# First layer of a two-layer attention and expert model on one core: q and k feature-major by head pairs, attention between projections, modulation sums on three engines and in layer two

## The reference, cut to what matters

```python
mod = c_act @ ada_w[layer] + ada_b[layer]            # 1024 x 6144 in each layer
sh_a, sc_a, g_a, sh_f, sc_f, g_f = split(mod, 6)
h = rmsnorm(x) * (1 + sc_a) + sh_a
# layer 0, 8 heads, two components of width 64 in each:
q, k, v = split(h @ w_qkv, 3)                        # each 512 x 1024
q, k = rmsnorm of every 64 columns, with gains
p[c] = softmax(q[c] @ k[c].T / 8 + bias[head], causal)
o = rmsnorm((p[0] - lam * p[1]) @ v) * (1 - lam_init)
x = x + g_a * (o @ w_o)
# layer 1: keys and values from their own modulation (kv_ada_w, 1024 x 2048), dilated attention
x = x + g_f * moe(rmsnorm(x) * (1 + sc_f) + sh_f)    # both layers: 2 of 32 experts for a token
```

## Time and profile before

| | us |
|---|---|
| median of 3 runs | 2227.99 |
| lowest, highest | 2224.74, 2230.22 |
| the profiled execution | 2229.98 |
| its span, first to last instruction | 2228.3 |

### The profile page before, as it was taken

The page is one execution under the profiler, slowest core; times in us unless marked ns, Lnnn a source line. Parts: engine busy times, 40 slices in busy tenths (PEclk is TensorE's granted clock), DMA queues, the critical chain, the costliest instruction groups (busy, mean ns, idle before and its releaser), DMA issues.

```text
span 2228.3 us, 16930 instructions
## 1 busy us (share of the span) xinstructions
PE 1804.4 (81%) x6253; PEld 825.3 (37%) x6253; DVE 694.2 (31%) x1078; ACT 449.1 (20%) x1002; POOL 131.5 (6%) x153
## 2 busy tenths in 40 slices
PE   1899767496899988998739999976869989998873
PEld 0433234345343333332224344443534433333321
DVE  5577567574100000000050255554330000000003
ACT  2111044302212111111030044441211111111100
POOL 0000010000100000000000000000000100000000
PEclk9999967696899999999969999996869999999996
DMA  7588730144699999999922112032038999999994
GB/s 279 205 332 308 263 118 19 60 151 165 220 351 394 392 388 384 391 380 391 396 103 76 38 38 76 26 126 97 38 125 304 398 395 387 388 379 381 392 389 176
DMA packets 243306, 552.62 MB, mean 248 GB/s; under 512 B 13328, under 2 KB 26209, under 8 KB 243222
## 3 DMA queue, kind: packets, MB, share of 16 engines
q1 hardware_dynamic: 221056, 501.24, 60.6%
q0 software_dynamic: 20624, 47.25, 6.0%
q10 hardware_dynamic: 1542, 3.01, 0.4%
HBM read 546.12 MB, written 32.59 MB: 260 GB/s over the span
## 4 chain that ended last, share of the span: by engine, by line
PE 55%; DMA 20%; DVE 14%; ACT 5%; issue 4%; SPq 0%; ACTq 0%; DVEq 0%; POOL 0%; POOLq 0%; PEldq 0%
PE psum L1818 22%; DMA ring<-in_moe_w_up_dram 17%; PE psum L1489 8%; PE psum L1849 7%; PE psum L1736 4%; PE psum L1535 4%; DVE W L1039 3%; PE psum L1561 2%; PE psum L1800 1%; ACT ring L715 1%; PE psum L1757 1%; DVE W L958 1%; DVE W L1126 1%; DVE small L1130 1%; PE psum L1455 1%
## 5 line engine op out<-in xcount | busy, mean ns | idle before, releaser
L1818 PE MATMUL psum<-ring,V 128*64 128x512 f32 (+1 forms) x2048 | 628.3, 630 | 92.8 <-DMA ring<-in_moe_w_up_dram 75.8
L1818 PEld LDWEIGHTS psum<-ring,V 128*64 128x64 f32 (+1 forms) x2048 | 239.8, 162 | 448.1 <-issue 447.9
L1849 PE MATMUL psum<-ring,V 128*64 128x512 f32 (+1 forms) x1024 | 305.5, 600 | 15.3 <-issue 10.4
L851 ACT ACTIVATE V<-psum,mods,scls 128x128 f32<-128x128 f32 x336 | 126.2, 456 | 525.8 <-PE psum L1800 525.8
L1489 PE MATMUL psum<-ring,HT 128*128 128x512 f32 x384 | 169.4, 596 | 0.0
L1849 PEld LDWEIGHTS psum<-ring,V 128*64 128x64 f32 (+1 forms) x1024 | 107.5, 154 | 157.7 <-issue 157.7
L1350 DVE TENSOR_TENSOR V<-V,psum 128x512 f32<-128x512 f32 x42 | 28.9, 688 | 408.0 <-PE psum L1818 408.0
L958 DVE SCALAR_TENSOR_TENSOR W<-ring,cact,W 128x512 f32<-128x512 f32 x196 | 147.4, 752 | 7.0
L1363 DVE COPY HT<-psum 128x512 f32<-128x512 f32 x42 | 29.1, 692 | 319.4 <-PE psum L1849 319.4
L1356 DVE COPY V<-psum 128x512 f32<-128x512 f32 x42 | 29.0, 691 | 290.5 <-PE psum L1829 290.5
L1039 DVE RECIPROCAL W<-W 128x512 f32<-128x512 f32 x24 | 80.5, 3353 | 115.3 <-ACT W L705 115.3
(11 more groups left out here) (253 smaller groups left out, 1508.7 us busy)
## 6 DMA issues: line engine op xcount, KB each, us to landing
ring<-in_moe_w_gate_dram SPq DMA_DIRECT2D x64, 2048.0 KB, 20.5
ring<-in_moe_w_up_dram SPq DMA_DIRECT2D x64, 2048.0 KB, 19.7
ring<-in_moe_w_down_dram SPq DMA_DIRECT2D x64, 2048.0 KB, 19.1
ring<-in_ada_w_dram SPq DMA_DIRECT2D x24, 2048.0 KB, 13.5
ring<-in_a_w_qkv_dram SPq DMA_DIRECT2D x6, 2048.0 KB, 19.3
ring<-in_kv_ada_w_dram SPq DMA_DIRECT2D x4, 2048.0 KB, 13.7
V<-expert_rows POOLq DMA_DIRECT2D x8, 1024.0 KB, 7.1
ring<-in_kv_w_dram SPq DMA_DIRECT2D x3, 2048.0 KB, 21.5
```

What stands on the lines that cost most here:

```text
L851: ins = act.activation(V[:, 2 * D + b * D + k * P:2 * D + b * D + (k + 1) * P], bank[0][:, q * P:(q + 1) * P], ACT.Identity, bias=mod[:, 2 ...
L1818: ins = pe.matmul(bank[2 + 2 * i + b][half * w:(half + 1) * w, :], V[:, col:col + w], slot3(x)[:, k, :], start=(k == 0), stop=(k == KC - 1))
L1849: ins = pe.matmul(bank[6 + hf][half * w:(half + 1) * w, :], V[:, col:col + w], slot3(x, 4)[:, k, hf * HALF:(hf + 1) * HALF], start=(k == 0 ...
```

## The change

**Before the loop.** SP no longer waits for the vectors. x is loaded by POOL's queue, first of all. Modulation blocks 0 to 3 are summed by TensorE: products of 32 columns by 512, four of them side by side in the columns of the array, then ACT copies the 128 x 512 and four products of one column each give the modulation as columns. All modulation goes this way now: the DRAM round trip and the row copies are gone. The bias rows go to DRAM and back without waiting for the modulation.

**Layer one** becomes 30 iterations n, written out. Iterations 0 to 23 have a unit each: for each pair of heads p (n = 6p to 6p+5) k and q of one head, two units of values, k and q of the other. q and k come out feature-major, as in layer two (mean square by a product, square root, reciprocal of 128 x 512), and never go to DRAM. Twenty attention steps of 512 score columns each (one or two (head, chunk) segments, `segments`) stand at n mod 6 = 3, 4, 0, 1, 2. A step's scores are made at n, its transposes at n+1, its values at n+2. There is one buffer for scores, one for probabilities and one for transposed ones. The per-head norm and the transposes of its outputs are done pair by pair, and parts of the output projection stand in iterations 24 to 28. Modulation blocks 4 to 19 are summed in the loop, ten by DVE and six by POOL (15 instructions for a block), each with its own accumulator; their products of one column stand at fixed iterations (`REDUCE_AT`).

**Layer two.** The remaining eight modulation blocks are loaded as 16 halves of 1024 x 256 into slot 5 and summed by DVE beside the 12 value units; `half_reduce` puts two products of one column each for a half in TensorE's queue.

**Gates.** POOL makes a diagonal of the gate's columns, a product with ones makes the row, ACT copies it; the DRAM broadcasts are gone.

The core of the diff; the removed code is the code before that the sections above name:

```diff
+UNITS0, STEPS0 = 24, 20
+SEGMENTS = [[(0, 3)], [(0, 2), (0, 0)], [(0, 1), (1, 1)], [(1, 2), (1, 0)], [(1, 3)]]
+STEP_AT = {6 * p + at: 5 * p + i for p in range(4) for i, at in enumerate((3, 4, 6, 7, 8))}
+
+
+N_MOD0 = 20
+N_HALF = 2 * (N_MOD - N_MOD0)
+ON_POOL = [5, 8, 10, 12, 14, 16]
+ON_DVE = [i for i in range(4, N_MOD0) if i not in ON_POOL]
+SUM_AT = dict(zip((0, 1, 2, 5, 8, 11, 14, 17, 20, 23), ON_DVE))
+REDUCE_AT = {at + 1: [i] for at, i in SUM_AT.items()}
+for at, i in zip((4, 7, 8, 10, 13, 16), ON_POOL):
+    REDUCE_AT[at] = REDUCE_AT.get(at, []) + [i]
+REDUCED = [i for at in sorted(REDUCE_AT) for i in REDUCE_AT[at]]
+HALVES_AT = [[i for i in range(N_HALF) if i * 3 // 4 == u] for u in range(12)]
...
+def segments(x):
+
+    out, at = [], 0
+    for half, c in SEGMENTS[x % 5]:
+        out.append((2 * (x // 5) + half, c, at, (c + 1) * P))
+        at += (c + 1) * P
+    return out
...
+    mods = [("mod", 0, i) for i in range(N_MOD0)]
+    order = mods[0:4] + [("kq", 0, 0), ("v", 0, 0)] + mods[4:7] + [("kq", 0, 1)] + mods[7:10] + [("kq", 0, 2)]
+    order += mods[10:13] + [("v", 0, 1)] + mods[13:15] + [("kq", 0, 3)] + mods[15:19] + [("wo", 0, 0)] + mods[19:]
+    order += [("wo", 0, 1)]
+    slots = [{"mod": i if i < 4 else (i - 4) % 3, "kq": (4, 3)[i % 2], "v": 5, "wo": 4 + i}[kind] for kind, _, i in order]
...
+    order += [("v", 1, 0), ("v", 1, 1), ("v", 1, 2)] + [("half", 1, i) for i in range(4)] + [("kq", 1, 0)]
+    slots += [0, 1, 2, 5, 5, 5, 5, 0]
+    order += [("half", 1, i) for i in range(4, 9)] + [("kq", 1, 1)] + [("half", 1, i) for i in range(9, N_HALF)]
+    slots += [5] * 5 + [1] + [5] * (N_HALF - 9)
+    order += [("kq", 1, i) for i in range(2, 2 * GROUPS)] + [("wo", 1, 0)]
+    slots += [2, 0, 1, 2, 0]
...
-            sp.wait_ge(vec_in, 16 * N_VEC)
...
+            pool.dma_start(x3, t["x"][0].rearrange("(c p) n -> p c n", p=P)).then_inc(x_in, 16)
...
+                def gate_diag(to, cols):
+
+                    pool.tensor_tensor(to.rearrange("p (k n) -> p k n", k=KC), ident.unsqueeze(1).broadcast_to([P, KC, P]),
+                                       cols.unsqueeze(2).broadcast_to([P, KC, P]), ALU.mult).then_inc(s["diag"].sem, 1)
...
+                    for j, i in enumerate(ON_POOL):
+                        n, acc = AT["mod", 0, i], ACC[1]
+                        arrived(pool, n)
+                        pool.wait_ge(mod_red, 4 if j == 0 else 4 + REDUCED.index(ON_POOL[j - 1]) + 1)
+                        step(pool.tensor_scalar(acc, slot3(n)[:, 0, :], cact[:, 0:1], None, ALU.mult))
+                        for k in range(1, KC):
+                            step(pool.tensor_scalar(slot3(n)[:, k, :], slot3(n)[:, k, :], cact[:, k:k + 1], None, ALU.mult))
+                            ins = pool.tensor_tensor(acc, acc, slot3(n)[:, k, :], ALU.add)
+                            if k < KC - 1:
+                                step(ins)
+                        ins.then_inc(mod_pool, 1)
...
-                gate_rows(V, 2 * D)
+                    pool.wait_ge(*s["added"](N_STEPS))
+                gate_diag(ga_diag[l], mods[l][:, 16:24])
...
+                    for n in range(UNITS0 + 6):
+                        if 1 <= n <= UNITS0 and (n - 1) % 6 not in (2, 3):
+                            tile_root(n - 1)
+                        if n < UNITS0 and n % 6 not in (2, 3):
+                            tile_square(n)
+                        if n == 1:
+                            for h in range(H):
+                                act.wait_ge(setup_pe, 4 + h)
+                                act.activation(T3[:, h, :], bank[(5, 7)[h % 2]], ACT.Identity).then_inc(setup_act, 1)
+                        if n >= 12 and n % 6 < 2:
+                            head_out(2 * (n // 6 - 2) + n % 6)
+                        if n - 2 in STEP_AT:
+                            step_out(STEP_AT[n - 2])
+                        if n - 1 in STEP_AT:
+                            step_probs(STEP_AT[n - 1])
+                        if n in STEP_AT:
+                            step_exps(STEP_AT[n])
+                        if n >= 11 and n % 6 == 5:
...
+                            sub_root(n // 6 - 1)
...
+                            step(dve.reciprocal(RS0, RS0))
+                            if p >= 2:
+                                dve.wait_ge(*s["s_pe"](5 * (p - 1) - (2 if head == 0 else 0)))
+                            gain = V_QG if kind else V_KG
+                            dve.scalar_tensor_tensor(tile0(p, head, kind), bank[n % 2], colV[:, gain:gain + 1], RS0,
+                                                     ALU.mult, ALU.mult).then_inc(s["proj_free"].sem, 1)
...
+                    def step_mix(x):
+                        segs = segments(x)
+                        dve.wait_ge(*s["exps"](x + 1))
+                        step(dve.reciprocal(small2[:, 4:4 + len(segs)], small2[:, 0:len(segs)]))
...
+                    for n in range(UNITS0 + 6):
+                        if 1 <= n <= UNITS0:
+                            unit_out(n - 1)
+                        if n - 1 in STEP_AT:
+                            step_mix(STEP_AT[n - 1])
+                        if n >= 11 and n % 6 == 5:
+                            sub_mean(n // 6 - 1)
+                        for i in REDUCE_AT.get(n - 1, []):
+                            mod_columns(i)
+                        if n in SUM_AT:
+                            i = SUM_AT[n]
+                            m = ON_DVE.index(i)
+                            arrived(dve, AT["mod", 0, i])
+                            dve.wait_ge(mod_red, 4 if m == 0 else 4 + REDUCED.index(ON_DVE[m - 1]) + 1)
+                            mod_sum_of(ACC[0], slot3(AT["mod", 0, i]), mod_sum)
+                        if n in STEP_AT:
+                            step_top(STEP_AT[n])
+                        if n >= 11 and n % 6 == 5:
+                            sub_norm(n // 6 - 1)
...
+                        for i in HALVES_AT[u]:
+                            dve.wait_ge(half_in[i % 2], 16 * (i // 2 + 1))
+                            if i >= 2:
+                                dve.wait_ge(mod_red, N_MOD0 + i - 1)
+                            mod_sum_of(HALF_ACC[i % 2], half_slot(i), mod_sum)
+                        if u:
+                            for i in HALVES_AT[u - 1]:
+                                half_columns(i)
+                    for i in HALVES_AT[11]:
+                        half_columns(i)
...
+                pe.wait_ge(mod_col, i if i < 4 else 4 + REDUCED.index(i))
+                for j in range(4):
+                    ins = pe.matmul(bank[6][:, 4 * i + j:4 * i + j + 1], acc[:, j * P:(j + 1) * P],
+                                    C[:, C_32:C_32 + 1] if i < 4 else ones[:, 0:1], start=True, stop=True)
+                ins.then_inc(mod_red, 1)
...
+                for r in range(2):
+                    for q in range(4):
+                        k = 4 * r + q
+                        ins = pe.matmul(bank[4 + i % 2][32 * q:32 * (q + 1), :], W[:, 2048 + 32 * k:2048 + 32 * (k + 1)],
+                                        slot3(n)[:, k, :], start=(r == 0), stop=(r == 1))
+                ins.then_inc(mod_pe, 1)
+                if i:
+                    mod_reduce(i - 1)
+            mod_reduce(3)
...
+                    def unit(n):
+                        p, j = divmod(n, 6)
+                        if n >= 2:
+                            pe.wait_ge(*s["proj_free"](n - 1))
...
+                                if k == 2 and n and j != 4:
+                                    tile_ms(n - 1)
...
+                    def step_scores(x):
+                        p = x // 5
+                        pe.wait_ge(*s["proj_free"](6 * p + (2 if x % 5 < 2 else 6)))
+                        pe.wait_ge(*s["added"](x))
...
+                    for n in range(UNITS0 + 6):
+                        if n < UNITS0:
+                            unit(n)
+                        elif n == UNITS0:
+                            tile_ms(n - 1)
+                        if n == 1:
+                            pe.wait_ge(hank_in, 16)
+                            for h in range(H):
+                                if h >= 2:
+                                    pe.wait_ge(setup_act, 1 + h)
+                                pe.matmul(bank[(5, 7)[h % 2]], flip, V[:, h * S:(h + 1) * S], start=True,
...
+                        if n >= 12 and n % 6 < 2:
+                            head_turn(2 * (n // 6 - 2) + n % 6)
+                        if n - 2 in STEP_AT:
+                            step_values(STEP_AT[n - 2])
+                        if n - 1 in STEP_AT:
+                            step_turn(STEP_AT[n - 1])
+                        if n in STEP_AT:
+                            step_scores(STEP_AT[n])
+                        for i in REDUCE_AT.get(n, []):
+                            mod_reduce(i)
+                        if n == 24:
```

(82 more changed lines are left out.)

776 lines of the change are left out of this document (300 added, 476 removed).

## The result

| | before | changed kernel |
|---|---|---|
| median | 2226.39 us (4 runs) | 2243.95 us (4 runs, 2241.39 to 2245.97) |
| ratio | | 1.0076, 95% interval 1.0058 to 1.0094 |
| span of the profiled execution | 2228.3 | 2242.7 |

The change makes the kernel 0.8% slower; forecast were 2207 and a gain. The time lies inside the stated range, on the other side of no change.

The account below looks back on a forecast made before the run. TensorE was busy for 81% of the span, so its idle time was where time could come from. Layer one's 70 us less and layer two's 49 more gave -21: 2207 us against the median, range 2166 to 2250.

Parts of the forecast that it names:

- Part 1: Up to layer one's first unit: it starts at 45 us, where it was 62.4; bounds 41 and 51.
- Part 2: Layer one's pairs of heads: engines wait in a ring, 78.9 us a pair against 65 of TensorE work; ends at 346.4.
- rival 1: Layer one's pairs: TensorE is the bound after all, 66 us a pair instead of 79, 2168; chance 0.16.
- rival 3: Layer one's ring: activation table loads cost more, 18 us less what overlaps, 2221; chance 0.06.
- rival 5: Layer one: half clock holds through the pairs, some 40 us more in each of three, 2320; chance 0.06.
- Part 3: Layer one from iteration 24 to the second norm: norm at 438.5 against 513.06, 74.6 us less.
- part 4: GpSimd's six modulation blocks in layer one: 17 us a block, 5 us cost together, leaving 70 us less.
- the step's rule for T: Layer one, T us per GpSimd block: TensorE has 15 us from iteration 7 to 8, so 17 costs about 2.
- Rival 4: Layer one: GpSimd's sums bound; with T us a block, TensorE waits at iterations 8 and 10; T = 40 gives 2250; chance 0.18.
- Part 5: Layer two's value units: waits for modulation columns add 37 us and lower clock 12, 49 more; bounds 20 and 58.
- The sum: Whole kernel: 70 us less in layer one and 49 more in layer two, -21, 2207.3 on the span.
- the parts costed at nothing: Reloading x, gate products in the router and GpSimd's later diagonal before layer two: claimed to cost nothing.

Follow-up runs that it names:

- experiment 5: Changed kernel with GpSimd doing only two of the 15 instructions of each of its six blocks: 2213.47 us.
- experiment 6: Changed kernel with GpSimd freeing each block after two instructions, then doing 14 on spare memory for five of six blocks, nobody waiting: 2228.98 us.
- experiment 7: Changed kernel with GpSimd doing 11 of the 15 instructions of each of its six blocks: 2234.23 us.
- experiment 8: Changed kernel with the mean square in layer two's tiles put back from k = 2 to k = 4: 2259.27 us.

## Why the prediction was wrong, step by step

**Part 1 held in its time, in part by luck.** First unit at 45.58, forecast 45. Its last release was another: the transposes were done at 43.2, 2 us before my sum, and the unit waited 2.4 us for the first q and k block, whose load I had not put on the path.

**Part 2 held once GpSimd is taken out.** In the changed kernel the first pair took 72 us, forecast 65, and the other three 93, 86 and 77 (iterations 5, 11, 17 and 23 end at 118, 211, 297 and 374), forecast 78.4, 79 and 79. The one in which GpSimd does nothing is the one that fits. With GpSimd nearly idle (experiment 5) the four take 70.1, 75.4, 77.8 and 75.1: together 298.5, where I had 299.4 without GpSimd's 1. That the sum is so near is luck in part, 5 too few in the first pair against 7 too many in the others. Two starts of scores in the last pair, 322.85 and 337.98, are 15.1 apart, as forecast:

```profile
308.14 1.16 PE psum L1520 x8
322.85 2.03 PE psum L1520 x8
337.98 1.75 PE psum L1520 x4
349.12 1.06 PE psum L1520 x4
359.47 1.07 PE psum L1520 x8
384.61 2.08 PE psum L1520 x8
```

Gaps of 14.7, 15.1, 11.1, 10.4 and 25.1 stand against 15.1, 15.1, 11.9, 10.4 and 26.4. So rival 1 (TensorE is the bound, 2168), rival 3 (dearer table loads) and rival 5 (half clock throughout) fall; the clock in the stage was 0.89.

**Part 3 held.** From 374 to the last output product's end near 461.2 are 87 us, forecast 88; the norm behind it takes 6.2, forecast 4.1. With GpSimd nearly idle (experiment 5) the transposes start at 437.7: the sum before part 4 gave 438.5.

**Part 4 is the first step that failed.** It put 5 us on GpSimd; experiment 5 puts 30.5. TensorE found waiting for GpSimd was a sign of being wrong that I had named. Two things went wrong. The block was 24 us and not 17: the instructions take 1692 and 1335 ns, where I took 1.1 with a wait, which no row of before gave. And the step's rule for T was only half of the cost. Rival 4's formula, T - 15 at iteration 8 and T - 22 at 10, gives 9 and 2 for T = 24, and the trace has waits of 10.8 and 1.7 us:

```profile
PE psum L1430 <- POOL W L517: 12.4, 2, 10.8
```

But "DVE's two-input instructions may be slowed beside it" stood there without a price of its own, and it is the other half: 15 us (experiment 6). Even at T near 17, where I had charged 5, the cost is 20.8 (experiment 7). So the sign did not turn at T = 29, as rival 4 had it, but well below: with blocks of 17 us the kernel is already 0.35% slower than before, with the rest of the change as it is.

**Part 5 was right in what it saw and missed a second cause.** With the loads out of the way the value units take 128.2 and 131.3 us; forecast were 119.4 and 12 for the clock, 131.4. The split is near too: the waits come to 27.9 and 29.8 us and the products of one column to 10.5 and 10.4, 38 and 40 together, where I had 37 for both, and the units' own products take 7 and 9 us longer at a clock of 0.89 and 0.88, where I had 12. What failed is that I read SP's queue for the first layer and not here. The list in which blocks are loaded puts a q and k block, whose slot comes free only with value unit 3 or 7, ahead of a half that is needed at once. That is 24 us on the span (155.6 against 131.4) and 25 in the runs.

**The sum missed a part.** The moved mean square in layer two's tiles, k = 2 for k = 4, stands in the whole diff and has no line in the sum. It is worth 14 to 15 us, in favour of the change.

Together: -21 as forecast, +25.5 for GpSimd, +24 to 25 for SP's queue, -14 to -15 for the mean square give +13.5 to +15.5; measured on the span +14.4, in the medians 17.6. Two costs of about the same size were missed, and a gain hid part of them. That the time still lies inside the stated range is this cancelling, and so luck: with the mean square where it was it is 2259.27 (experiment 8), outside. Of the parts costed at nothing none was tried by itself: from the second norm's transposes to the experts it is 2.5 us less than before (59.2 to 56.7), from the experts to the first value unit 2.0 more (54.2 to 56.2), and I leave both open.

## What to carry to other kernels

Work given to an idle engine is not free for the busy one: ask whether the busy one's instructions take two inputs from the on-chip memory while the other reads it, and price the slower instructions as well as the wait for the result. An in-order load queue has to be read for each stage: a block whose slot is not free yet holds all that stand behind it, however early their own places are free. And go through a diff number by number: here one `2` for a `4` gave back 14 of the 50 us that the two missed costs took.

## What the runs showed of the hardware

In the changed kernel GpSimd takes 1692 ns in the mean for a multiplication by a scalar and 1335 ns for an addition of 512 columns in float32; undisturbed they are at 1.57 and 1.28 us in the chain above. DVE needs 752 for its two-in-one instruction of that size (the kernel before). The figure of the Trainium skill, GPSIMD Engine Reference, section 3.1, gave an estimate of 1.1 us for the addition (my division by four), so the trace has more.

DVE is slowed by kind of operand. While GpSimd reads and writes SBUF, the on-chip memory outside the matmul banks (PSUM), an instruction whose two inputs both lie there goes from 758 to 1050 ns (L961) and from 619 to 1063 ns (L1012, 384 columns); one with one of its two inputs in PSUM (L1000, 752 ns, and 751 in experiment 5) and the reciprocal (3349 and 3350 ns) stay as they are. GpSimd pays too, 1.9 us for some of its multiplications in place of 1.57:

```profile
117.37 7.87 DVE L961 SCALAR_TENSOR_TENSOR W<-ring,cact,W 128x512 f32<-128x512 f32 x7
...
119.34 1.88 POOL L516 TENSOR_SCALAR ring<-ring,cact 128x512 f32<-128x512 f32 x1
```

Seven of DVE's instructions take 7.87 us there, 5.47 in experiment 5. The Trainium skill, SBUF — State Buffer, section "Who interferes with whom", says that a DVE instruction with two SBUF inputs contends with a GpSimd instruction that reads SBUF, and that one with at most one SBUF input does not, outside the modes in which DVE uses two ports. The trace agrees for the instructions named so far; it would have been the rule to weigh in part 4. DVE's multiplication by a scalar, the first of each sum (L959), has one of its tensors in SBUF and is slower all the same in some executions: its mean over 45 to 270 us is 481 ns in experiment 5, 539 in the changed kernel and 668 in experiment 6, the longest 489, 746 and 1087. In which mode it runs no run here shows.
